# Gate and up products in 32-token groups on four column strips, with VectorE turning the activations

## The chip, the core and the metric

The kernel runs on one core of a Trainium2 chip. The time is that of one execution on the device in microseconds, and a kernel's time is the median of its runs. All arithmetic is float32.

## What is computed

One layer over 1024 latent tokens of width 1024: a mixer (a linear recurrence and gated linear attention), a LayerNorm, and then the part that matters here, a mixture of 32 experts of which each token takes 4:

```python
logits = xt @ w_router + b_router
top_v, top_i = lax.top_k(logits, 4);  top_w = softmax(top_v)
# for the tokens of expert e:
gate = min(xb @ w_gate[e] + b_gate[e], 7)
up   = clip(xb @ w_up[e] + b_up[e], -7, 7)
act  = (up + 1) * gate * sigmoid(1.702 * gate)
y    = (act @ w_down[e] + b_down[e]) * row_weight      # added to the token's row
```

Each of w_gate[e], w_up[e] and w_down[e] is 1024 x 1024, 4 MB. The last LayerNorm follows.

## The kernel before

The mixer, the router and the construction of the job table take the first 669 us of the profile. Then comes the expert loop, with which the change deals.

**Jobs.** A job is up to 128 tokens of one expert. The table is built on the chip. Job u has a type from 1 to 4, the number of quarters (32 tokens) in use; `J_FIRST` says that it is the first job of its expert, and `J_ORD` the expert's ordinal. An expert's first job is the partial one; jobs of type 4 with the same weights may follow. For these inputs there are 49 jobs of 32 experts. By the matmuls of the trace their types are, from u = 0: 4 4 3 2 4 2 4 3 | 1 4 2 3 2 4 4 1 | 3 2 2 4 1 3 4 3 | 2 4 4 1 4 4 3 3 | 2 1 4 1 4 4 4 1 | 4 4 4 2 4 2 4 1 | 4. The jobs 1, 4, 6, 9, 13, 14, 19, 25, 26, 28, 34, 36, 37, 40, 44, 46 and 48 are later jobs of their expert; the other 32 are first.

**TensorE.** Its order in iteration u is: first half of gate_up(u), the turn of the activations of u-1, second half of gate_up(u), down(u-1). `gate_up` multiplies the turned tokens `xT` (the stationary operand) with eight pieces of weights `ring[0..7]` (1 MB each; even ones gate, odd ones up, two k tiles of 128 rows in each). It waits for each piece by itself (`d_gu[q]`) and gives it back by itself (`gu_used`). The code for the tokens depends on the type: "full" (128 stationary columns, 512 moving ones), "half" (64 columns, two matmuls side by side on two column strips), "quarter" (32 columns, four matmuls of 256 side by side on four strips); type 3 is half and then quarter. Gate sums lie in PSUM banks 0 and 1, up sums in 2 and 3. `turn` is 2 to 8 transposes on TensorE into banks 4 and 5, which ScalarE (line 1258) and VectorE (line 1870) copy to `aT`. `down` multiplies `aT` with four pieces `ring[8..11]` of w_down into banks 6 and 7, again by full, half or quarter.

**VectorE.** In iteration u: the copy of `aT`; `turn_rows_in` (line 1671, a 32x32 block transpose of the gathered tokens, after the last use of `xT`); `swiglu(u)` (lines 1698 to 1713; bias adds out of PSUM first, which give the banks back through `g_biased` and `gu_free`, one instruction per part of 32 or 64 partitions); `weigh(u-1)` (lines 1645 to 1658) after down(u-1). ScalarE has the sigmoid (line 1270).

**GpSimd.** Gathers the tokens, scatters the results with an add, and spreads the bias rows of an expert over 128 partitions (`partition_broadcast`: line 2039 for gate and up, line 2042 for down).

**SyncE's queue.** In iteration u, in this order: if job u+1 is the first of its expert, its two bias rows and its eight pieces, piece q as soon as gate_up(u) has used its buffer (line 497); if job u is first, its down bias and its four pieces of w_down, piece q as soon as down(u-1) has used it (line 525). The ring holds one expert, so each piece has one buffer.

Of the kernel before, what the change touches and what calls it, by code (L numbers as in the profile page):

```python
# [13 lines left out]
ALU = mybir.AluOpType  # L14
# [23 lines left out]
def layer(nc, x, c, ctx, c_ctx, w_ada, b_ada, w_in, conv_w, conv_b, lru_wa, lru_ba, lru_wx, lru_bx,  # L38
# [28 lines left out]
    GUP, DNP = 8, 4  # L67
# [12 lines left out]
    with ctxs:  # L80
# [162 lines left out]
        ebias = reg(o, 3, D); o += 3072  # L243
        assert o <= AW
        xacc = reg(16384, 2, D)
        brow = adarow[0:1, 0:3, :].rearrange("p a b -> p (a b)")
# [12 lines left out]
        psG, psU = psall[:, 0:2 * BANK], psall[:, 2 * BANK:4 * BANK]  # L259
        psT, psY = psall[:, 4 * BANK:6 * BANK], psall[:, 6 * BANK:8 * BANK]  # L260
# [4 lines left out]
        JOB_KINDS = {4: (FULL, 0, D), 3: (HALF + QUARTER, 0, BANK + QW), 2: (HALF, 0, BANK), 1: (QUARTER, BANK, BANK + QW)}  # L265
# [43 lines left out]
        d_bias, d_bdn, bias_spread, bdn_spread = sem("d_bias"), sem("d_bdn"), sem("bias_spread"), sem("bdn_spread")  # L309
# [4 lines left out]
        act_turned, aT_act, aT_dve = sem("act_turned"), sem("aT_act"), sem("aT_dve")  # L314
# [115 lines left out]
        def _(sp):  # L430
# [90 lines left out]
            def dn_pieces(e, u):  # L521
                for q in range(DNP):
                    sp.wait_ge(dn_used, DNP * u + (q + 1))
                    w_v = w_down[0].rearrange("e (q c p) n -> e q p c n", c=2, p=P)[:, q]
                    sp.dma_start(ring[GUP + q], w_v[ds(e, 1)].rearrange("a p c n -> p (a c) n")).then_inc(d_dn[q], 16)

            def bias_rows(e):
                for g, b_v in enumerate((b_gate, b_up)):
                    sp.dma_start(brow[:, g * D:(g + 1) * D], b_v[0][ds(e, 1)]).then_inc(d_bias, 16)

            def down_row(e):
                sp.dma_start(brow[:, 2 * D:3 * D], b_down[0][ds(e, 1)]).then_inc(d_bdn, 16)
# [5 lines left out]
            with sp.Fori(0, OUTER) as o4:  # L538
                live = sp.value_load(tab[0:1, ds(o4 * (INNER * NC) + J_LIVE, 1)], min_val=0, max_val=1)
                with sp.If(live > 0):  # L540
                    with sp.Fori(0, INNER) as i4:
                        u = o4 * INNER + i4
                        nxt = sp.value_load(tab[0:1, ds(u * NC + (2 * NC + J_FIRST), 1)], min_val=0, max_val=1)
                        with sp.If(nxt > 0):
                            e = sp.value_load(tab[0:1, ds(u * NC + (2 * NC + J_E), 1)], min_val=0, max_val=NE - 1)
                            spread = sp.value_load(tab[0:1, ds(u * NC + (NC + J_ORD), 1)], min_val=16, max_val=16 * NE)
# [3 lines left out]
                            gu_pieces(e, u)  # L550
# [18 lines left out]
        def gate_up(pe, kind, u, order_, k0, k1, first=False):  # L569
            if k0 == 0:  # L570
                pe.wait_ge(xT_ready, u + 1)
            sweeps = {4: ("full",), 3: ("half", "quarter"), 2: ("half",), 1: ("quarter",)}[kind]
            for sweep in sweeps:
                for q in range(k0, k1):
                    g = q % 2
                    if q < 2 and sweep == sweeps[0]:
                        if g == 0 and not first:
                            pe.wait_ge(g_biased, u)
                        if g == 1:
                            pe.wait_ge(gu_free, u + 1)  # L580
                    if sweep == sweeps[0]:
                        pe.wait_ge(d_gu[q], order_)
                        if kind < 4:
                            settle(pe)
                    for k in (2 * (q // 2), 2 * (q // 2) + 1):
                        w = ring[q][:, k % 2]
                        if sweep == "full":
                            for s in range(2):
                                mm = pe.matmul(ps[2 * g + s], xT[:, k, :], w[:, s * BANK:(s + 1) * BANK],  # L589
                                               start=(k == 0), stop=(k == KD - 1))  # L590
                        if sweep == "half":
                            for j in range(2):
                                mm = pe.matmul(ps[2 * g][HT * j:HT * j + HT, :], xT[:, k, 0:HT], w[:, j * BANK:(j + 1) * BANK],  # L593
                                               start=(k == 0), stop=(k == KD - 1), skip_group_check=True)
                        if sweep == "quarter":
                            r = slice(QUARTER_AT[kind], QUARTER_AT[kind] + QR)
                            for j in range(4):
                                mm = pe.matmul(ps[2 * g + 1][QR * j:QR * j + QR, 0:QW], xT[:, k, r], w[:, j * QW:(j + 1) * QW],  # L598
                                               start=(k == 0), stop=(k == KD - 1), skip_group_check=True)
                    if sweep == sweeps[-1]:  # L600
                        mm.then_inc(gu_used, 1)

        def down(pe, kind, u, order_):
            pe.wait_ge(aT_act, u + 1)
            pe.wait_ge(aT_dve, u + 1)
            pe.wait_ge(y_biased, u + 1)
            sweeps = {4: ("full",), 3: ("half", "quarter"), 2: ("half",), 1: ("quarter",)}[kind]
            for sweep in sweeps:
                for k in range(KD):
# [9 lines left out]
                    if sweep == "half":  # L619
                        for j in range(2):  # L620
                            mm = pe.matmul(ps[6][HT * j:HT * j + HT, :], aT[:, k % 4, HT * (k // 4):HT * (k // 4) + HT],  # L621
                                           w[:, j * BANK:(j + 1) * BANK],
                                           start=(k == 0), stop=(k == KD - 1), skip_group_check=True)
# [31 lines left out]

# [1491 lines left out]
```

## Time and profile before

| what | value |
|---|---|
| median of 3 runs | 2295.06 us (2294.68 to 2297.74) |
| the profiled execution | 2291.36 us, its span 2289.3 us |
| TensorE matmul busy | 2155.0 us, 94% |
| VectorE / ScalarE / GpSimd busy | 45% / 21% / 20% |
| weights and all else moved | 512.34 MB, mean 224 GB/s |

The page's busy shares are means over the whole span. The expert loop runs from 669 us to 2270 us. In the chain of waits each row is work that the end waited for; in the timeline, the number in brackets is how long the engine stood idle before the row and what ended that. A float32 matmul shows as two records.

### The profile page before, as it was taken

To read this page: it belongs to the slowest core of one execution; us is meant where nothing else is said; L and a number is where in the kernel's file an instruction comes from. 1 tells how busy PE (TensorE), PEld (TensorE's weight loads), DVE (VectorE), ACT (ScalarE), POOL (GpSimd) and SP (SyncE) were. 2 spreads that over 40 slices of the span, in tenths; PEclk is the share of its full clock that TensorE was granted. 3 is DMA by queue.
4 is the path that set the end of the run, shared out by engine and by line. 5 is a ranking of instruction groups with operands and counts; after the bars stand their busy time and mean duration, and the time that the engine had idled before them with its cause. 6 is when DMAs were issued, how large, how long until landed. Compare 5 with 4: busy or idle time off the path is not lost.

```text
span 2289.3 us, 35330 instructions
## 1 busy us (share of the span) xinstructions
PE 2155.0 (94%) x9863; PEld 998.5 (44%) x9864; DVE 1023.8 (45%) x1586; ACT 479.0 (21%) x647; POOL 465.4 (20%) x427
## 2 busy tenths in 40 slices
PE   6999999789959999999998899999999999999995
PEld 3544444554544444443443344444443444444442
DVE  2765656557782442444335343333254332222346
ACT  2343347422210111111111111111111111111134
POOL 1011100202311221223122232212113212212212
PEclk9999999789969999999999999999999999999998
DMA  9222320032256767789479999747899648897673
GB/s 351 84 69 70 101 74 19 1 114 83 83 194 213 270 246 239 249 332 374 158 281 401 340 369 403 255 163 254 306 371 348 236 160 271 296 314 247 204 283 128
DMA packets 169785, 512.34 MB, mean 224 GB/s; under 512 B 16815, under 2 KB 51383, under 8 KB 168586
## 3 DMA queue, kind: packets, MB, share of 16 engines
q1 hardware_dynamic: 152290, 468.96, 54.9%
q0 software_dynamic: 15840, 37.45, 7.4%
q10 hardware_dynamic: 1608, 5.29, 0.6%
q8 instruction: 30, 0.49, 0.1%
q14 instruction: 17, 0.14, 0.0%
HBM read 482.08 MB, written 32.51 MB: 225 GB/s over the span
## 4 chain that ended last, share of the span: by engine, by line
PE 86%; DVE 6%; DMA 3%; SPq 2%; issue 2%; ACT 1%; POOLq 0%; DVEq 0%; POOL 0%; ACTq 0%
PE psall L589 27%; PE psall L617 14%; PE psall L593 10%; PE psall L774 9%; PE psall L621 5%; PE psall L598 4%; PE psall L762 3%; PE psall L881 2%; PE psall L875 2%; DMA arena<-in_w_down_dram 2%; PE psall L626 2%; PE psall L658 1%; PE psall L741 1%; SPq L438 1%; DVE arena L1498 1%
## 5 line engine op out<-in xcount | busy, mean ns | idle before, releaser
L589 PE MATMUL psall<-arena 128*128 128x512 f32 x1472 | 645.1, 596 | 23.7 <-issue 18.9
L589 PEld LDWEIGHTS psall<-arena 128*128 128x128 f32 x1472 | 278.4, 191 | 368.8 <-issue 362.4
L617 PE MATMUL psall<-arena 128*128 128x512 f32 x736 | 322.6, 596 | 5.2 <-issue 2.8
L593 PE MATMUL psall<-arena 128*64 128x512 f32 x1152 | 256.1, 595 | 6.2 <-DMA arena<-in_w_up_dram 2.1
L1671 DVE STREAM_TRANSPOSE arena<-arena 128x1024 f32<-128x1024 f32 x49 | 61.0, 1245 | 446.7 <-PE psall L589 276.5
L774 PE MATMUL psall<-arena 128*128 128x512 f32 (+1 forms) x560 | 227.1, 562 | 0.0
L617 PEld LDWEIGHTS psall<-arena 128*128 128x128 f32 x736 | 139.2, 191 | 183.0 <-issue 181.2
L1258 ACT COPY arena<-psall 128x512 f32<-128x512 f32 x49 | 28.7, 586 | 724.5 <-PE psall L658 724.5
L1870 DVE COPY arena<-psall 128x512 f32<-128x512 f32 x48 | 33.2, 691 | 313.7 <-PE psall L658 307.1
L1270 ACT ACTIVATE arena<-arena 128x1024 f32<-128x1024 f32 x49 | 51.8, 1057 | 571.1 <-DVE arena L1698 571.1
L1991 POOL DMA_INDIRECT arena<-h_rows,lruw x144 | 147.6, 1025 | 82.6 <-POOL lruw L1984 39.7
L1653 DVE TENSOR_TENSOR arena<-psall,arena 32x256 f32<-32x256 f32 (+2 forms) x122 | 78.6, 645 | 189.0 <-PE psall L617 137.2
L593 PEld LDWEIGHTS psall<-arena 128*64 128x64 f32 x1152 | 83.2, 137 | 162.6 <-issue 162.6
L774 PEld LDWEIGHTS psall<-arena 128*128 128x128 f32 x560 | 106.3, 190 | 109.1 <-issue 106.1
L1984 POOL COPY lruw<-arena 128x4 int32 (+1 forms) x48 | 9.2, 191 | 658.2 <-DVE arena L1671 620.2
L621 PE MATMUL psall<-arena 128*64 128x512 f32 x576 | 129.3, 595 | 13.4 <-DMA arena<-in_w_down_dram 11.1
L598 PE MATMUL psall<-arena 128*32 128x256 f32 x2048 | 117.3, 381 | 1.9 <-issue 1.9
L2005 POOL DMA_INDIRECT stream_rows<-arena,lruw x56 | 91.6, 1636 | 93.6 <-DMA stream_rows<-arena,lruw 44.9
L1658 DVE SCALAR_TENSOR_TENSOR arena<-arena,lruw,adarow 32x256 f32<-32x256 f32 (+2 forms) x122 | 90.8, 744 | 6.6
L598 PEld LDWEIGHTS psall<-arena 128*32 128x32 f32 x2048 | 64.0, 110 | 59.7 <-issue 22.2
L621 PEld LDWEIGHTS psall<-arena 128*64 128x64 f32 x576 | 41.7, 137 | 97.8 <-issue 97.8
L2039 POOL PARTITION_BROADCAST arena<-adarow x31 | 75.3, 2428 | 29.4 <-issue 16.2
(336 smaller groups left out, 2120.7 us busy)
## 6 DMA issues: line engine op xcount, KB each, us to landing
arena<-in_w_gate_dram SPq DMA_DIRECT2D x128, 1024.0 KB, 6.7
arena<-in_w_up_dram SPq DMA_DIRECT2D x128, 1024.0 KB, 7.4
arena<-in_w_down_dram SPq DMA_DIRECT2D x128, 1024.0 KB, 9.2
arena<-in_w_ada_dram SPq DMA_DIRECT2D x16, 1024.0 KB, 5.2
arena<-in_w_ada_dram SPq DMA_DIRECT2D x4, 2048.0 KB, 14.5
arena<-in_x_dram SPq DMA_DIRECT2D x16, 512.0 KB, 7.0
arena<-in_w_in_dram SPq DMA_DIRECT2D x16, 512.0 KB, 4.1
arena<-in_w_out_dram SPq DMA_DIRECT2D x1, 4096.0 KB, 13.9
```

The costliest lines, as they stand in the source:

```text
L589: mm = pe.matmul(ps[2 * g + s], xT[:, k, :], w[:, s * BANK:(s + 1) * BANK], start=(k == 0), stop=(k == KD - 1))
L593: mm = pe.matmul(ps[2 * g][HT * j:HT * j + HT, :], xT[:, k, 0:HT], w[:, j * BANK:(j + 1) * BANK], start=(k == 0), stop=(k == KD - 1), skip ...
L598: mm = pe.matmul(ps[2 * g + 1][QR * j:QR * j + QR, 0:QW], xT[:, k, r], w[:, j * QW:(j + 1) * QW], start=(k == 0), stop=(k == KD - 1), skip ...
L617: mm = pe.matmul(ps[6 + s], aT[:, k, :], w[:, s * BANK:(s + 1) * BANK], start=(k == 0), stop=(k == KD - 1))
L621: mm = pe.matmul(ps[6][HT * j:HT * j + HT, :], aT[:, k % 4, HT * (k // 4):HT * (k // 4) + HT], w[:, j * BANK:(j + 1) * BANK], start=(k == ...
L762: mm = pe.matmul(ps[i % JB][:, :], uT[:, k, j * P:(j + 1) * P], wv[:, k, :], start=(k == 0), stop=(k == KD - 1))
L774: mm = pe.matmul(ps[i % JB][0:w, 0:seg[1] - seg[0]], wring[n % WRING][:, k, 0:w], uT[:, k, seg[0]:seg[1]], start=(k == 0), stop=(k == KD - 1))
L1653: mm = dve.tensor_tensor(yb[p0:p1, c:c + n], psY[p0:p1, c:c + n], ebias[p0:p1, 2, b:b + n], ALU.add)
L1658: mm = dve.scalar_tensor_tensor(out=yb[p0:p1, c:c + n], in0=yb[p0:p1, c:c + n], scalar=(wcolq if c else wcol)[p0:p1], in1=adarow[p0:p1, 3, ...
L1991: pool.indirect_dma_start(out=xg[:, CW * t:CW * (t + 1)], out_offset=None, in_=h2_dram.rearrange("a (j n) -> (a j) n", n=CW), in_offset=ba ...
L2005: return pool.indirect_dma_start(out=to, out_offset=bass.IndirectOffsetOnAxis(ap=index, axis=0), in_=yb[:, cols], in_offset=None, bounds_c ...
L2039: pool.partition_broadcast(ebias[:, 0:2].rearrange("p a n -> p (a n)"), brow[:, 0:2 * D]).then_inc(bias_spread, 16)
```

## The change

`gate_up` has one form for all types. Tokens go in groups of 32: group t has the stationary columns 32t to 32t+31 and PSUM bank t. Each matmul has 512 moving columns, 256 of gate and 256 of up, and four of them stand side by side on four column strips. The loop over k runs in two sweeps of four k tiles; a sweep waits for four pieces at once, runs the groups in use (nested tests on the type) and gives the four back together. `gate_up` waits for `gu_free` (both bias adds of the job before) ahead of its first matmul; `g_biased` is no longer waited for there.

The turn on TensorE and the copies by ScalarE and VectorE are gone. VectorE turns the activations by 32x32 blocks, straight to `aT`, after `weigh(u-1)`; w_down's rows are read in another order to match (two adjacent rows, 8 KB, for each partition and piece).

The bias adds of `swiglu` are one instruction each for all types. The bias rows of gate and up come by DMAs that write 128 partitions; they are issued behind the eight pieces and a wait for `gu_free`, and GpSimd spreads only the down bias.

```diff
 def gu_pieces(e, u):
     for q in range(GUP):
-        if u is not None:
-            sp.wait_ge(gu_used, GUP * u + (q + 1))
+        if u is not None and q % 4 == 0:
+            sp.wait_ge(gu_used, NPAIR * u + (q // 2 + 2))
         ...
 def dn_pieces(e, u):
     for q in range(DNP):
         sp.wait_ge(dn_used, DNP * u + (q + 1))
-        w_v = w_down[0].rearrange("e (q c p) n -> e q p c n", c=2, p=P)[:, q]
+        w_v = w_down[0].rearrange("e (p q c) n -> e q p c n", q=DNP, c=2)[:, q]
 ...
 def bias_rows(e):
     for g, b_v in enumerate((b_gate, b_up)):
-        sp.dma_start(brow[:, g * D:(g + 1) * D], b_v[0][ds(e, 1)]).then_inc(d_bias, 16)
+        rows = b_v[0][ds(e, 1)].rearrange("a (j n) -> (a j) n", j=4)
+        sp.dma_start(ebq[:, g], rows.unsqueeze(1).to_broadcast([4, QR, QW])).then_inc(d_bias[g], 16)
 ...
-                            sp.wait_ge(bias_spread, spread)
-                            settle(sp)
-                            bias_rows(e)
                             gu_pieces(e, u)
+                            sp.wait_ge(gu_free, u + 2)
+                            bias_rows(e)
 ...
+        def gate_up(pe, groups, u, order_, m0, m1):
+            if m0 == 0:
+                pe.wait_ge(xT_ready, u + 1)
+                pe.wait_ge(gu_free, u + 1)
+            for m in range(m0, m1, 2):
+                for q in range(2 * m, 2 * m + 4):
+                    pe.wait_ge(d_gu[q], order_)
+                    settle(pe)
+                def group(t):
+                    for k in range(2 * m, 2 * m + 4):
+                        for j in range(4):
+                            mm = pe.matmul(psGU[QR * j:QR * j + QR, t], xT[:, k, QR * t:QR * t + QR],
+                                           wpair[k // 2][:, :, k % 2, QW * j:QW * j + QW],
+                                           start=(k == 0), stop=(k == KD - 1), skip_group_check=True)
+                    return mm
+                with pe.If(groups > 1):
+                    with pe.If(groups > 2):
+                        with pe.If(groups > 3):
+                            group(3)
+                        group(2)
+                    group(1)
+                group(0).then_inc(gu_used, 2)
 ...
 def down(pe, kind, u, order_):
-    pe.wait_ge(aT_act, u + 1)
-    pe.wait_ge(aT_dve, u + 1)
+    pe.wait_ge(aT_ready, u + 1)
     pe.wait_ge(y_biased, u + 1)
 ...
-                            by_kind(pe, t, lambda kind: gate_up(pe, kind, u, on_, 0, GUP // 2))
+                            with pe.If(t > 0):
+                                gate_up(pe, t, u, on_, 0, NPAIR)
                             tp, op_ = typ_of(pe, typ_p), ord_of(pe, ord_p, wait_p)
-                            with pe.If(tp > 0):
-                                pe.wait_ge(act_ready, u + 1)
-                                by_kind(pe, tp, lambda kind: turn(...).then_inc(act_turned, 1))
-                            by_kind(pe, t, lambda kind: gate_up(pe, kind, u, on_, GUP // 2, GUP))
                             by_kind(pe, tp, lambda kind: down(pe, kind, u, op_))
 ...
+        def swiglu(u, groups):
+            dve.wait_ge(gu_used, u * NPAIR + NPAIR)
+            dve.wait_ge(d_bias[0], order_)
+            dve.tensor_tensor(gv, psGU[:, 0:groups, 0], bias[0], ALU.add).then_inc(g_biased, 1)
+            dve.wait_ge(d_bias[1], order_)
+            dve.wait_ge(aT_ready, u + 1)
+            dve.scalar_tensor_tensor(out=uv, in0=psGU[:, 0:groups, 1], scalar=1.0, in1=bias[1],
+                                     op0=ALU.add, op1=ALU.add).then_inc(gu_free, 1)
 ...
+        def turn_activations(u, groups):
+            dve.wait_ge(act_ready, u + 2)
+            dve.wait_ge(dn_used, u * DNP + DNP)
+            dve.transpose(aT[:, :, 0:QR * groups].rearrange("p b (t s) -> p t b s", s=QR),
+                          ub[:, 0:QW * groups].rearrange("p (t i b) -> p t b i", i=QR, b=KD)).then_inc(aT_ready, 1)
 ...
                                     by_kind(dve, tp, lambda kind: weigh(u, kind, orderp))
+                                    by_kind(dve, typ_of(dve, typ_c), lambda groups: turn_activations(u, groups))
```

## Rows read from the trace of the kernel before

**Rows 1.** The page: busy time, and the chain that ended last, by engine.

```profile
PE 2155.0 (94%) x9863; PEld 998.5 (44%) x9864; DVE 1023.8 (45%) x1586; ACT 479.0 (21%) x647; POOL 465.4 (20%) x427
...
PE 86%; DVE 6%; DMA 3%; SPq 2%; issue 2%; ACT 1%; POOLq 0%; DVEq 0%; POOL 0%; ACTq 0%
```

**Rows 2.** The expert loop's TensorE groups by form: busy, mean ns, idle before and releasers.

```profile
L589 PE MATMUL psall<-arena 128*128 128x512 f32 x1472 | 645.1, 596 | 23.7 <-issue 18.9 <-DVE arena L1698 4.8
...
L593 PE MATMUL psall<-arena 128*64 128x512 f32 x1152 | 256.1, 595 | 6.2 <-DMA arena<-in_w_up_dram 2.1 <-issue 1.7 <-DVE arena L1698 0.8
L621 PE MATMUL psall<-arena 128*64 128x512 f32 x576 | 129.3, 595 | 13.4 <-DMA arena<-in_w_down_dram 11.1 <-issue 2.2
...
L658 PE MATMUL psall<-ident,arena 128*128 128x128 f32 x288 | 41.0, 278 | 2.5 <-DVE arena L1713 2.5
```

**Rows 3.** The chain in order of time: start, us, what (jobs 29 to 31).

```profile
1597.84 13.97 PE psall L589 x32
1612.68 13.74 PE psall L589 x32
...
1640.15 7.02 PE psall L593 x32
1647.17 3.59 PE psall L598 x64
```

**Rows 4.** The page's group of the quarter's weight loads.

```profile
L598 PEld LDWEIGHTS psall<-arena 128*32 128x32 f32 x2048 | 64.0, 110 | 59.7 <-issue 22.2
```

**Rows 5.** TensorE's timeline behind quarter sweeps (jobs 8 and 9).

```profile
964.40 7.09 PE L621 MATMUL psall<-arena 128*64 128x512 f32 x32 [1.53 <-issue]
...
976.01 13.97 PE L589 MATMUL psall<-arena 128*128 128x512 f32 x32 [0.93 <-issue]
```

**Rows 6.** What SyncE's queue waited for: total, times, longest.

```profile
SPq L497 <- PE psall L589: 446.2, 125, 33.5
```

**Rows 7.** Line 497 (the pieces) from 1845 to 1875 us, time to landing.

```profile
DMA to landing us min/median/max: 4.8/5.2/5.8
```

**Rows 8.** TensorE's timeline from 1259 to 1278 us; five like rows lie between.

```profile
1259.86 1.94 PE L593 MATMUL psall<-arena 128*64 128x512 f32 x8 [0.61 <-DMA arena<-in_w_up_dram]
...
1277.53 1.94 PE L621 MATMUL psall<-arena 128*64 128x512 f32 x8 [1.01 <-DMA arena<-in_w_down_dram]
```

**Rows 9.** Busy time by stretch, the granted clock, DMA share and GB/s.

```profile
8.00:14.00 6.00, 1.52 (x9) 0.44 (x13) 1.57 (x3) 1.40 (x2) 2.63 (x4) 1.00 1.01 419
...
1220.00:1230.00 10.00, 9.21 (x46) 3.57 (x46) 9.02 (x15) 2.99 (x3) 2.38 (x1) 1.00 1.03 405
```

**Rows 10.** VectorE's groups by form.

```profile
L1671 DVE STREAM_TRANSPOSE arena<-arena 128x1024 f32<-128x1024 f32 x49 | 61.0, 1245 | 446.7 <-PE psall L589 276.5 <-PE psall L598 97.5 <-PE psall L593 61.0
...
L1658 DVE SCALAR_TENSOR_TENSOR arena<-arena,lruw,adarow 32x256 f32<-32x256 f32 x64 | 31.4, 491 | 1.7
L1658 DVE SCALAR_TENSOR_TENSOR arena<-arena,lruw,adarow 64x512 f32<-64x512 f32 x36 | 31.1, 864 | 2.3
...
L1698 DVE TENSOR_TENSOR arena<-psall,arena 128x1024 f32<-128x1024 f32 x23 | 27.3, 1187 | 1.1 <-PE psall L589 1.1
...
L1653 DVE TENSOR_TENSOR arena<-psall,arena 32x256 f32<-32x256 f32 x64 | 26.9, 420 | 2.4 <-issue 1.6
...
L1653 DVE TENSOR_TENSOR arena<-psall,arena 64x512 f32<-64x512 f32 x36 | 24.8, 689 | 49.4 <-PE psall L626 27.4 <-POOLq L2067 15.7 <-PE psall L621 5.4
```

**Rows 11.** TensorE's timeline at the second job and at the end of the loop.

```profile
712.86 16.50 PE L589 MATMUL psall<-arena 128*128 128x512 f32 x32 [4.49 <-DVE arena L1698]
...
2251.22 1.09 PE L658 MATMUL psall<-ident,arena 128*128 128x128 f32 x8 [2.48 <-DVE arena L1713]
2253.91 15.67 PE L617 MATMUL psall<-arena 128*128 128x512 f32 x32 [1.60 <-ACT arena L1260]
```

**Rows 12.** TensorE's busy time and granted clock behind the wait ahead of 712.86.

```profile
714.00:718.00 4.00, 4.00 (x6) 0.51 0.45 145
```

**Rows 13.** Waits of VectorE for GpSimd between 1640 and 1800 us.

```profile
DVE arena L1653 <- POOLq L2067: 15.7, 2, 9.7
```

More of the change, by code:

```diff
@@ L242, in layer @@
         yb = reg(o, D); o += 1024
-        ebias = reg(o, 3, D); o += 3072
+        ebq = reg(o, 2, QW); o += 512
+        ebd = reg(o, D); o += 1024
         assert o <= AW
         xacc = reg(16384, 2, D)
-        brow = adarow[0:1, 0:3, :].rearrange("p a b -> p (a b)")
+        wpair = [reg(4096 * m, 2, 2, D) for m in range(NPAIR)]
+        brow = adarow[0:1, 2, :]
         mod2 = ada1[:, :, :, :].rearrange("p a b c -> p (a b c)")[:, 0:2 * KD].rearrange("p (s k) -> p s k", s=2)
@@ L566, in _ @@
             sp.wait_ge(late_out, 48)
-        def gate_up(pe, kind, u, order_, k0, k1, first=False):
-            if k0 == 0:
+        def gate_up(pe, groups, u, order_, m0, m1):
+            if m0 == 0:
                 pe.wait_ge(xT_ready, u + 1)
[L572 to L601, printed above, removed]
@@ L620, in down @@
                         for j in range(2):
[L621 removed]
+                            mm = pe.matmul(ps[6][HT * j:HT * j + HT, :], aT[:, k, 0:HT],
                                            w[:, j * BANK:(j + 1) * BANK],
@@ L654, in ord_of @@
             return eng.snap(bounded, min_val=16, max_val=16 * NE)
-        def turn(pe, src, n, first=0):
-            for k in range(first, n):
-                mm = pe.transpose(psT[:, k * P:(k + 1) * P], src[:, k * P:(k + 1) * P], ident[:, :])
-            return mm
         @block.tensor
@@ L976, in _ @@
             t0, o0 = typ_of(pe, typ_p), ord_of(pe, ord_p, wait_p)
-            by_kind(pe, t0, lambda kind: gate_up(pe, kind, 0, o0, 0, GUP // 2, True))
+            gate_up(pe, t0, 0, o0, 0, NPAIR // 2)
             job_lists()
-            by_kind(pe, t0, lambda kind: gate_up(pe, kind, 0, o0, GUP // 2, GUP))
+            gate_up(pe, t0, 0, o0, NPAIR // 2, NPAIR)
             with pe.Fori(0, OUTER) as o4:
@@ L1641, in weigh @@
             def weigh(u, kind, order_):
-                parts, lo, hi = JOB_KINDS[kind]
+                parts = DOWN_PARTS[kind]
                 dve.wait_ge(y_dve, u + 1)
@@ L1690, in finish @@
                                          op0=ALU.mult, op1=ALU.add).then_inc(fin_ready, 1)
-            def swiglu(u, kind):
-                parts, lo, hi = JOB_KINDS[kind]
+            def swiglu(u, groups):
                 s7 = 1.0 / (1.0 + math.exp(-SWIGLU * LIMIT))
-                dve.wait_ge(gu_used, u * GUP + GUP)
-                dve.wait_ge(bias_spread, order_)
-                for p0, p1, c, b, n in parts:
-                    mm = dve.tensor_tensor(gb[p0:p1, c:c + n], psG[p0:p1, c:c + n], ebias[p0:p1, 0, b:b + n], ALU.add)
-                mm.then_inc(g_biased, 1)
-                for p0, p1, c, b, n in parts:
-                    mm = dve.scalar_tensor_tensor(out=ub[p0:p1, c:c + n], in0=psU[p0:p1, c:c + n], scalar=1.0,
-                                                  in1=ebias[p0:p1, 1, b:b + n], op0=ALU.add, op1=ALU.add)
-                mm.then_inc(gu_free, 1)
-                w = slice(lo, hi)
+                w = slice(0, QW * groups)
+                gv, uv = (v[:, w].rearrange("p (t n) -> p t n", t=groups) for v in (gb, ub))
+                bias = [ebq[:, g].unsqueeze(1).to_broadcast([P, groups, QW]) for g in range(2)]
+                dve.wait_ge(gu_used, u * NPAIR + NPAIR)
[5 more added lines that the diff above has]
+                                         op0=ALU.add, op1=ALU.add).then_inc(gu_free, 1)
                 dve.wait_ge(gu_free, u + 2)
@@ L1916, in _ @@
                                     dve.nop()
+                                dve.nop()
+                            with dve.Else():
+                                by_kind(dve, typ_of(dve, typ_c), lambda groups: turn_activations(u, groups))
                                 dve.nop()
```

57 lines of the change are left out of this document (17 added, 40 removed).

## The prediction, made before the changed kernel ran

> **What bounds the kernel now.** I read the page first: TensorE is busy 94% of the span, and the chain that ended last is TensorE's for 86% [rows 1]. The other engines lie beside it. Then the groups by form: the first group of the expert loop waits 23.7 us, of which one "issue" of 13.5 us precedes the loop, the half forms wait 19.6 us, and 13.2 of these are named as DMA's; for more than 1000 us of matmuls TensorE hardly stands [rows 2]. The chain in order of time shows the loop as matmul blocks end to end [rows 3]. This could mislead: an expert's 12 MB take about as long as a small job's matmuls, so I looked at what SyncE's queue waits for. It is TensorE's use of the buffers [rows 6]: one buffer per piece, so the moment at which a piece is given back decides when the next expert's comes. Between 1200 and 1280 us, where experts with one small job follow each other, DMA is full and the waits for it lie [rows 8, 9]. So there are two bounds: TensorE over most of the loop, DMA in runs of small jobs.
>
> **TensorE's work.** A half gate_up of a full job is 32 records in 13.74 us, 429 ns for each pass of 512 columns. The half form takes 7.02 us for 16 such passes of two strips, 439 ns; the quarter form 3.59 us for 16 passes of 256 columns on four strips, 224 ns, that is 11 ns over half of 427 [rows 3]. The new form has four strips and 512 columns: 427 + 11 = 438 ns, like the half form. A group is 16 passes, 7.02 us, so gate_up is 28.08 us for type 4 (before 27.46), 21.06 for 3 (21.22), 14.04 for 2 (14.04), 7.02 for 1 (7.18). With 23, 8, 10 and 8 jobs: +14.3 - 1.3 - 1.3 = **+11.7 us**. These are 2304 passes, so the bounds are far: 429 ns a pass, as in the full form, makes it 21 us less, and 448 ns 23 us more. I take the row with strips, since it is the nearest.
>
> The turns go. Their group is 41.0 us busy [rows 2], but overlaps its neighbours at both ends; between two halves the chain loses 1612.68 - 1597.84 - 13.97 = 0.87 us for eight transposes [rows 3], and 0.2 to 1.0 for the others. Summed over the 48 turns inside the loop: **-35 us** (bounds -30 and -41).
>
> Full-width and strip matmuls now alternate in every pair of jobs. A block after another width shows 13.97 instead of 13.73 us [rows 3]; for 23 full downs I take 0.2 us ahead and 0.15 behind, less those that had it before, and less 0.2 where a full gate_up followed a strip down: **+2.5 us** (0 to 8). The Trainium skill says that changing the tiling mode drains TensorE (TensorEngine Tiling (Array Packing), Key Properties); the trace agrees, with these 0.2 us.
>
> Behind quarter sweeps TensorE stands 0.2 to 1.5 us for "issue" [rows 5]: 28 ns an instruction leaves its sequencer no lead at a jump. The new groups run at 55 ns an instruction; the waits ahead of down go, those after a quarter down stay, and the nested tests there cost, by my guess, 0.15 us more each; no row shows them. 16 x 0.5 saved, 16 x 0.15 added: **-5.6 us** (-8 to +5). Sum of TensorE's own work: 11.7 - 35 + 2.5 - 5.6 = **-26 us**.
>
> **When the weights come.** A piece asked for with idle engines lands after 4.8 us [rows 7]. In a full stretch, seven waits in a row end within 1277.53 - 1259.86 = 17.67 us, 2.9 us a piece [rows 8], gathers and scatters included; at 405 GB/s [rows 9] a piece (1.05 MB) alone is 2.6. I take 2.8 us a piece and, at the same rate, 0.33 us of DMA time for each quarter (128 KB) that a job gathers, and again for its scatter. With these I kept an account of the 49 jobs: blocks of TensorE by the durations above, each piece in the queue when its buffer is free, landed 2.8 us after the one before, and a block not before its pieces. By the rules of before it finds 17 us of waits in the right places (jobs 17, 18 and 32, 33), and runs parallel to the ends of the blocks in the trace within some 2 us. So it may be trusted with the new rules.
>
> Before, piece q came back after q/8 of gate_up; now four after the first half and four at the end. The second lot is asked for when gate_up(u) ends, and its last piece lands 4.8 + 3 x 2.8 = 13.2 us later. TensorE needs it after down(u-1) and half of gate_up(u+1). Job 35 (type 1, behind a down of type 1): 3.6 + 0.8 + 3.5 = 7.9 us, so it waits **5.3**. Jobs 20 and 47: 7.0 + 3.5, **2.7** each. Job 10: 11.4, **1.8**. After a full down (13.8 us) nothing waits. Sum 12.5, before none.
>
> The runs: take 15 to 18. From the end of job 15's gate_up TensorE has 14.0 + 21.1 + 4.3 = 39.4 us of work ahead of job 17's first sweep. DMA must by then bring what is left of job 16's eight pieces (6.7, as the first lot was asked for 3.5 us before), four of w_down and the first four of job 17: 14.7 x 2.8 = 41.2, + 1.4 to land, + 3.4 for gathers and scatters: 46.0. Wait 6.6. Before, the first matmul there needed one piece of the four, not all. Carried on: 20.6 us of waits in jobs 17 and 18; 4.2 in job 12; 7.8 in jobs 22 and 24; 15.5 in jobs 32 and 33. Sum 48 us, before 17. DMA has no less to move there, so these runs keep nothing of TensorE's gain, and begin later.
>
> Together 60.5 against 17: **+43 us**. I take off half of what w_down might gain: it now moves 8 KB per partition at a stretch; in the one stretch that loads 8 KB rows (w_ada) the rate was 419 GB/s against 405 [rows 9], some 4% of a third of the pieces, 4.5 us in the account, where it binds; half: **-2 us**. The new bias DMAs (256 packets of 1 KB for each expert) stand in the account with 0.6 us.
>
> **The edges.** gate_up(u+1) now needs both bias adds: turn_rows_in 1.25 and two adds of 1.19 us, with semaphores 3.9 us after gate_up(u) [rows 10], against a down of 3.6 at least: 0.2 us in five places, +1, and +1.2 at job 1, where TensorE already waits 4.49 us [rows 11]. At the last job the swiglu ends at 2251.2; the turn must now wait for weigh(47), 4 x 0.42 + 4 x 0.49 + 0.2 = 3.8 us [rows 10], and then takes 1.25: down(48) at 2256.3 instead of 2253.9 [rows 11]: +2.4. Elsewhere the turn is covered: weigh (3.8 us for a quarter, 6.9 with two halves of 0.69 and 0.86 besides) and turn (1.25 us for all, less for fewer groups; double if its strided read halves the rate) against a gate_up of 7 us at least, 14 behind most downs of type 3. If that cover went, down would wait. The bias adds of types 1 to 3, GpSimd's broadcast and the copies lie beside TensorE: 0. **+4 us**.
>
> **The sum.** -26 + 43 - 2 + 4 = +19. Some waits fall where TensorE is late anyhow; with all of it in one account the total is 3 us less: **+16 us**.
>
> After the wait of 4.49 us the granted clock was 0.51 for 4 us, the level of 1.2 GHz, and the block took 16.50 us instead of 13.9 [rows 11, 12]. Waits of 5 us and more come five times now; two precede work that decides: up to +5, in the range only.
>
> Own time 2291.4 + 16 = 2307.4; the median of the runs is 3.7 above the profiled execution: **2311 us**.
>
> **Rivals.**
> *The lots flow faster (ends faster).* Asked for four at a time, pieces come at 2.6 us instead of 2.8. For: 419 GB/s in [rows 9] is 2.5 us; the queue never runs dry within a lot. Against: with the queue full in the loop, it came to 405 GB/s and 2.9 us a piece [rows 8, 9]. At 2.6 us the account gives 23 us less, so -7: **2288**; it decides below 2.67 us a piece. Chance 0.20.
> *Gain and waits cancel.* 2.7 us a piece gives 14 us less, passes of 430 ns some 16 (2304 x 8 ns, less what waits take back): +2 or 0, **2297**. Chance 0.15.
> *VectorE is late with aT.* weigh(u-1) may wait for GpSimd's scatter, 9.7 us once [rows 13], and the turn now stands behind it. It decides where gate_up(u+1) is of type 1 (eight jobs), from a lateness of some 3 us on; with 3 us beyond that in five of them +15: **2326**. Against: GpSimd loses 2.4 us of broadcast per expert. Chance 0.08.
> *The loads of the weights are not covered.* The quarter form has 64 loads of 110 ns within 3.59 us [rows 3, 4], so they overlap there. If at 512 columns they cost 27 ns more a pass (as one 110 ns load in four): 2304 x 27 = +62, less some 20 of waits that vanish: **2353**. Chance 0.04. The Trainium skill has a rule of this kind, that a weight load overlaps a running matmul only if it is for other rows of the array (TensorE: Matmul & The Clock Gate, Part 3); all four strips use the same rows, yet the rows above show the overlap.
> My forecast has 0.53.
>
> **The numbers.** The forecast's own range is 2301 to 2323. With the rivals, VectorE's included and the loads left out: 2284 to 2327. A change within 0.2% (4.6 us) can't be told from none. Faster: the first rival, 0.20; the same: the second, 0.15; slower: forecast, VectorE, loads, 0.65.
>
> **What would show it.** Gate_up blocks of 28.1 us for type 4 and 7.0 per group; no line 658; waits of TensorE for w_gate and w_up of 40 to 60 us in sum (jobs 12, 17, 18, 22, 33, 35, 47), ended by DMA; DMA idle early in each gate_up; down(48) some 2.4 us later. The prediction is wrong if the DMA waits sum to under 30 us (the first rival), if a pass is not 438 ns, or if down waits for VectorE's turn in the middle of the loop.

## The result

| kernel | median | runs |
|---|---|---|
| before | 2294.87 us | 2294.48 to 2297.74 |
| changed | 2371.26 us | 2370.16 to 2373.26 |

The ratio is 1.0331, 95% interval [1.0313, 1.0349]: 76.4 us slower. Slower was the side that I gave 0.65, but the time lies 44 us beyond the range.

### The profile page after: what moved, and what is told of

Read it like the earlier page. It is cut to its first block, busy times and chain, and to the rows that moved or that the text cites. A ratio compares the mean times of both kernels' runs of the same rounds, so it can differ in the third digit from the quotient of the medians.

```text
span 2371.5 us, 42832 instructions
## 1 busy us (share of the span) xinstructions
PE 2147.2 (91%) x14119; PEld 853.9 (36%) x14120; DVE 977.9 (41%) x1439; ACT 388.4 (16%) x549; POOL 391.2 (16%) x395
## 2 busy tenths in 40 slices
DMA packets 161716, 520.39 MB, mean 219 GB/s; under 512 B 17007, under 2 KB 59767, under 8 KB 144138
## 4 chain that ended last, share of the span: by engine, by line
PE 73%; DMA 12%; DVE 6%; SPq 5%; issue 2%; ACT 1%; DVEq 0%; POOLq 0%; POOL 0%
PE psall L582 37%; PE psall L608 12%; PE psall L761 9%; DMA arena<-in_w_up_dram 8%; DMA arena<-in_w_down_dram 4%; PE psall L749 3%; PE psall L868 2%; PE psall L612 2%; PE psall L862 2%; SPq L499 2%; PE psall L728 1%; SPq L532 1%; SPq L440 1%; DVE arena L1474 1%; PE psall L618 1%
## 5 line engine op out<-in xcount | busy, mean ns | idle before, releaser
L582 PE MATMUL psall<-arena 128*32 128x512 f32 x9216 | 1032.7, 607 | 111.2 <-DMA arena<-in_w_up_dram 73.0
L582 PEld LDWEIGHTS psall<-arena 128*32 128x32 f32 x9216 | 313.4, 112 | 818.7 <-issue 818.5
L1647 DVE STREAM_TRANSPOSE arena<-arena 128x1024 f32<-128x1024 f32 x49 | 61.0, 1245 | 807.4 <-PE psall L582 796.5
L608 PE MATMUL psall<-arena 128*128 128x512 f32 x736 | 323.9, 598 | 10.0 <-DVE arena L1694 8.7
L608 PEld LDWEIGHTS psall<-arena 128*128 128x128 f32 x736 | 138.4, 191 | 195.4 <-issue 183.9
L612 PE MATMUL psall<-arena 128*64 128x512 f32 x576 | 131.1, 597 | 19.3 <-DMA arena<-in_w_down_dram 18.7
L761 PEld LDWEIGHTS psall<-arena 128*128 128x128 f32 x560 | 106.3, 190 | 109.1 <-issue 106.1
L612 PEld LDWEIGHTS psall<-arena 128*64 128x64 f32 x576 | 40.1, 136 | 109.9 <-issue 109.8
L1694 DVE STREAM_TRANSPOSE arena<-arena 128x1024 f32<-128x1024 f32 (+3 forms) x49 | 76.5, 1562 | 1.0
L1980 POOL COPY lruw<-lruw 128x1 int32 x40 | 7.4, 184 | 417.3 <-DVE arena L1634 381.4
L749 PE MATMUL psall<-arena 128*128 128x512 f32 x160 | 70.0, 592 | 0.0
L1941 POOL TENSOR_TENSOR arena<-arena 128x1280 f32<-128x1280 f32 x8 | 23.2, 2904 | 268.6 <-ACT arena L1071 268.6
L618 PE MATMUL psall<-arena 128*32 128x256 f32 x1024 | 60.1, 380 | 1.5 <-issue 0.8
L868 PE MATMUL psall<-arena 128*128 128x512 f32 x128 | 59.3, 618 | 0.0
```

What stands on the lines that cost most here:

```text
L582: mm = pe.matmul(psGU[QR * j:QR * j + QR, t], xT[:, k, QR * t:QR * t + QR], wpair[k // 2][:, :, k % 2, QW * j:QW * j + QW], start=(k == 0) ...
L608: mm = pe.matmul(ps[6 + s], aT[:, k, :], w[:, s * BANK:(s + 1) * BANK], start=(k == 0), stop=(k == KD - 1))
L612: mm = pe.matmul(ps[6][HT * j:HT * j + HT, :], aT[:, k, 0:HT], w[:, j * BANK:(j + 1) * BANK], start=(k == 0), stop=(k == KD - 1), skip_gro ...
L618: mm = pe.matmul(ps[7][QR * j:QR * j + QR, 0:QW], aT[:, k, r], w[:, j * QW:(j + 1) * QW], start=(k == 0), stop=(k == KD - 1), skip_group_c ...
L749: mm = pe.matmul(ps[i % JB][:, :], uT[:, k, j * P:(j + 1) * P], wv[:, k, :], start=(k == 0), stop=(k == KD - 1))
L761: mm = pe.matmul(ps[i % JB][0:w, 0:seg[1] - seg[0]], wring[n % WRING][:, k, 0:w], uT[:, k, seg[0]:seg[1]], start=(k == 0), stop=(k == KD - 1))
```

## The profile after

The page, with the chain of waits by engine below the busy times:

```profile
span 2371.5 us, 42832 instructions
...
PE 2147.2 (91%) x14119; PEld 853.9 (36%) x14120; DVE 977.9 (41%) x1439; ACT 388.4 (16%) x549; POOL 391.2 (16%) x395
...
DMA packets 161716, 520.39 MB, mean 219 GB/s; under 512 B 17007, under 2 KB 59767, under 8 KB 144138
...
PE 73%; DMA 12%; DVE 6%; SPq 5%; issue 2%; ACT 1%; DVEq 0%; POOLq 0%; POOL 0%
...
L582 PE MATMUL psall<-arena 128*32 128x512 f32 x9216 | 1032.7, 607 | 111.2 <-DMA arena<-in_w_up_dram 73.0
...
L608 PE MATMUL psall<-arena 128*128 128x512 f32 x736 | 323.9, 598 | 10.0 <-DVE arena L1694 8.7
...
L612 PE MATMUL psall<-arena 128*64 128x512 f32 x576 | 131.1, 597 | 19.3 <-DMA arena<-in_w_down_dram 18.7
...
L618 PE MATMUL psall<-arena 128*32 128x256 f32 x1024 | 60.1, 380 | 1.5 <-issue 0.8
```

TensorE's share of the chain falls from 86% [rows 1] to 73%; DMA rises from 3 to 12%, SyncE's queue from 2 to 5%. The bytes moved are 520.39 MB for 512.34: 8 MB or 1.6% more, the 32 x 256 KB of the bias DMAs. What grew is the idle time ahead of the loop's matmuls. Before, the four groups of [rows 2] and three smaller ones had 54.0 us, 13.5 of them ahead of the loop, so 40; now it is 111.2 + 10.0 + 19.3 + 1.5, less 14.6 ahead of the loop: 127 us. The forecast had +47 of such waits (43 for weights, 4 at the edges), and +87 came.

TensorE's timeline from 1245 to 1315 us, where small jobs of new experts follow each other; rows between are left out:

```profile
1248.13 9.98 PE L582 MATMUL psall<-arena 128*32 128x512 f32 x64 [10.40 <-DMA arena<-in_w_up_dram]
1259.09 7.07 PE L582 MATMUL psall<-arena 128*32 128x512 f32 x64 [0.98 <-DMA arena<-in_w_up_dram]
...
1285.60 10.02 PE L582 MATMUL psall<-arena 128*32 128x512 f32 x64 [6.65 <-DMA arena<-in_w_up_dram]
1296.63 7.07 PE L582 MATMUL psall<-arena 128*32 128x512 f32 x64 [1.00 <-DMA arena<-in_w_up_dram]
...
1314.99 27.67 PE L582 MATMUL psall<-arena 128*32 128x512 f32 x256 [0.72 <-issue]
```

These are jobs 17 and 18, of type 2. Each has one long wait for pieces, ahead of its first sweep, and the same 64 matmuls that take 7.07 us take 10.0 behind it. The windows say why (us, busy time of PE, weight loads, VectorE, ScalarE and GpSimd, granted clock, DMA share, GB/s):

```profile
1244.00:1248.00 4.00, 0.00 (x0) 0.00 (x0) 1.13 (x1) 0.00 (x0) 1.82 (x2) 0.50 1.02 410
1248.00:1252.00 4.00, 3.87 (x20) 0.99 (x24) 0.00 (x0) 0.00 (x0) 0.00 (x0) 0.50 1.06 378
1252.00:1256.00 4.00, 4.00 (x32) 1.00 (x28) 0.00 (x0) 0.00 (x0) 0.00 (x0) 0.74 0.81 301
```

While TensorE stands, the granted clock falls to 0.50, the level of 1.2 GHz, and it is back only some 6 us after the work is (0.74 is the mean of 0.50 and full speed in the last window). A wait of 10 us costs 13.

SyncE's queue from 1273 to 1290 us, each row one DMA and how long its issue held the queue:

```profile
1273.77 2.84 SPq L499 DMA_DIRECT2D arena<-in_w_gate_dram  x1
1276.70 2.38 SPq L499 DMA_DIRECT2D arena<-in_w_up_dram  x1
1279.33 2.22 SPq L532 DMA_DIRECT2D arena<-in_b_gate_dram  x1
1281.65 4.66 SPq L532 DMA_DIRECT2D arena<-in_b_up_dram  x1
...
1289.73 2.98 SPq L527 DMA_DIRECT2D arena<-in_w_down_dram  x1
```

The two bias DMAs, 256 KB, held the queue for 6.9 us in this full stretch, more than the 5.2 us of the two 1 MB pieces ahead of them. That is not the 0.6 us of my account. What they do by themselves can be seen where the queue runs dry behind them:

```profile
761.00:763.00 2.00, 2.00 (x6) 0.90 (x5) 0.00 (x0) 0.00 (x0) 0.00 (x0) 1.00 0.94 368
763.00:765.00 2.00, 2.00 (x15) 0.47 (x17) 1.09 (x1) 0.00 (x0) 0.00 (x0) 1.00 0.30 103
765.00:767.00 2.00, 2.00 (x24) 0.65 (x20) 1.89 (x3) 0.00 (x0) 0.07 (x1) 1.00 0.09 29
```

The pieces end at 368 GB/s; then the last 103 x 2 + 29 x 2 = 264 KB, about the size of the two bias DMAs, trickle at a third of that and less, and the share of the DMA engines that are busy, the number ahead of the GB/s, is 0.30 and 0.09. Why these packets don't fill the 16 engines isn't said there: their size, their number and the source (each kilobyte is read 32 times) are new at once. Nor does the profile say how much of the 76 us hangs on it.

## The experiments

Two suspects were left: the lots of four pieces (the forecast's +43) and the bias DMAs (the forecast's 0.6). The first four runs take them one by one.

**Four sweeps of two k tiles.** Waits and releases by two pieces in place of four.

```diff
-if u is not None and q % 4 == 0:
-    sp.wait_ge(gu_used, NPAIR * u + (q // 2 + 2))
+if u is not None and q % 2 == 0:
+    sp.wait_ge(gu_used, NPAIR * u + (q // 2 + 1))
 ...
-for m in range(m0, m1, 2):        # q, k in range(2 * m, 2 * m + 4)
+for m in range(m0, m1):           # q, k in range(2 * m, 2 * m + 2)
```

> The changed kernel with four sweeps of two k tiles instead of two sweeps of four: each sweep waits for two pieces and gives two back. Theory A (the coarse lots cost what is missing): the waits for w_gate and w_up, 73 us in the changed kernel, fall by more than half, and the time by 30 to 45 us, to about 2330. Theory B (something else in the weight traffic, the bias DMAs or the order of w_down's rows, makes DMA slower): the waits stay above 50 us and the time falls by less than 15.

2325.27 us, ratio 1.0138 [1.0118, 1.0158]: 46 us less than the changed kernel. The group's idle time says where:

```profile
L582 PE MATMUL psall<-arena 128*32 128x512 f32 x9216 | 1016.5, 599 | 76.3 <-DMA arena<-in_w_up_dram 40.9 <-issue 23.5 <-DVE arena L1678 11.9
...
L612 PE MATMUL psall<-arena 128*64 128x512 f32 x576 | 134.5, 613 | 20.0 <-DMA arena<-in_w_down_dram 19.9
```

The waits for w_up fall by 32 us; those for w_down, which come behind the bias DMAs in the queue, stay. The time met the 30 to 45 us of theory A; the waits for w_up fell by 44%, not by more than half. Lots are a cause, but not alone.

**The bias DMAs behind w_down's pieces.**

```diff
 gu_pieces(e, u)
-sp.wait_ge(gu_free, u + 2)
-bias_rows(e)
 ...
 dn_pieces(ed, u)
+sp.wait_ge(gu_free, u + 2)
+bias_rows(eb)                     # where the next job has a new expert
```

> The changed kernel with one step of SyncE's queue moved: the two bias DMAs of the next expert are issued behind the four pieces of w_down, not ahead of them. Theory C (a bias DMA of 256 small rows holds SyncE's queue for up to 7 us while the queue is full, and w_down's issue behind it comes late): 15 to 30 us faster, about 2350. Theory A: within 5 us of the changed kernel.

2357.88 us, ratio 1.0273 [1.0253, 1.0293]: 13 us less, between the marks of the two theories (15 to 30, and under 5). Now w_down hardly waits (2.5 us), but w_up waits 81.9 instead of 73.0. The place in the queue decides who waits for the bias DMAs, not whether.

**The bias DMAs cut down.**

```diff
-sp.dma_start(ebq[:, g], rows.unsqueeze(1).to_broadcast([4, QR, QW]))
+sp.dma_start(ebq[0:4, g], rows)
```

> The changed kernel, but the bias DMAs write four partitions instead of 128 (the other partitions keep what was there, so the bias of gate and up is left out there). It takes both the hold of the queue and the DMA work of 8 MB in 1 KB packets away. Theory C: like bias_last or some 5 us better. If the 1 KB packets themselves are what slows the full stretches (360 GB/s against 398 before), it is 10 us and more better than bias_last.

2307.39 us, ratio 1.0055 [1.0036, 1.0074]: 64 us less, in one line, and 50 us less than with the bias DMAs behind w_down. It leaves out the gate and up biases in 124 of 128 partitions. The groups:

```profile
L582 PE MATMUL psall<-arena 128*32 128x512 f32 x9216 | 1018.4, 601 | 87.6 <-DMA arena<-in_w_up_dram 50.7 <-issue 28.9 <-DVE arena L1678 8.0
...
L612 PE MATMUL psall<-arena 128*64 128x512 f32 x576 | 127.8, 596 | 0.6 <-DMA arena<-in_w_down_dram 0.6
```

Against the changed kernel, 23.6 and 18.7 us of waits are gone, and 14.3 and 3.3 us of busy time of the same matmuls too: the clock lost behind the waits. Together 60 of the 64 us.

**w_down's rows in the old order.** The old `rearrange` of `dn_pieces`, 4 KB rows.

> The changed kernel with w_down read in the order of before, 4 KB rows, two for a partition (so the rows don't match the turned activations: the last product has its rows in another order). Theory D (8 KB rows 32 KB apart come slower than 4 KB rows that follow each other): 10 to 25 us faster. My prediction: 2 to 4 us slower.

2374.75 us, ratio 1.0353 [1.0335, 1.0371]. The 8 KB rows may be worth 3.5 us; the intervals overlap, so no more than a hint.

Then, why 256 KB cost so much.

**The same packets from distinct rows.** Each of the 128 packets of 1 KB reads a kilobyte of its own.

```diff
-rows = b_v[0][ds(e, 1)].rearrange("a (j n) -> (a j) n", j=4)
-sp.dma_start(ebq[:, g], rows.unsqueeze(1).to_broadcast([4, QR, QW]))
+rows = (w_gate, w_up)[g][0][ds(e, 1), 0:QR].rearrange("a r (j n) -> (a r j) n", j=4)
+sp.dma_start(ebq[:, g], rows)
```

> The changed kernel, but each bias DMA reads 128 different pieces of 1 KB (32 rows of the expert's w_gate or w_up, so the biases are other numbers) instead of four pieces 32 times each. Size, number and target of the packets stay. If the size and number of packets make the bias DMAs dear, it stays at about 2371. If it is that 32 packets read the same kilobyte, it comes near to bias_small, about 2310.

2315.61 us, ratio 1.0087 [1.007, 1.0104]. Same bytes, same size and number of packets, same places written: 56 of the 64 us are gone. Where the queue runs dry, the tail is short:

```profile
763.00:765.00 2.00, 2.00 (x18) 0.55 (x20) 1.39 (x2) 0.00 (x0) 0.00 (x0) 1.00 0.14 47
765.00:767.00 2.00, 2.00 (x24) 0.65 (x20) 2.00 (x2) 0.00 (x0) 0.19 (x1) 1.00 0.00 0
```

So it is neither the size of the packets nor their count. But two things differ between these DMAs: the changed kernel's read each kilobyte 32 times, and they name their source as four rows (`[4, QR, QW]`), the others as 128. At the first expert the pair of bias DMAs has the queue to itself. From 671 to 676 us, in slices of 0.125 us, the share of the 16 DMA engines that are busy, in tenths (9 is 90% and more), in the changed kernel and then here:

```profile
DMA  0000000002001122222222231222272222110000
DMA packets 266, 0.29 MB, mean 57 GB/s; under 512 B 8, under 2 KB 264, under 8 KB 264
```

```profile
DMA  0000086479959930050000000000000000000000
DMA packets 290, 0.29 MB, mean 57 GB/s; under 512 B 32, under 2 KB 288, under 8 KB 288
```

The changed kernel's pair keeps a quarter of the engines busy, about four of 16, for 3 us; the pair from distinct rows keeps up to 90% and more busy and is through in half of that. The small packets say the same: 8 for two DMAs, four each, against 32, 16 each. In windows of half a microsecond (the last three numbers are the granted clock, the DMA share and the GB/s):

```profile
673.00:673.50 0.50, 0.00 (x0) 0.00 (x0) 0.50 (x1) 0.00 (x0) 0.00 (x0) 0.50 0.26 94
```

```profile
672.00:672.50 0.50, 0.00 (x0) 0.00 (x0) 0.47 (x2) 0.00 (x0) 0.00 (x0) 0.50 0.86 256
```

An engine that is busy moves 94 / (0.26 x 16) = 23 GB/s in the first and 256 / (0.86 x 16) = 19 in the second. So the repeated reading itself does not slow it here; the DMA is slow because it runs on about four engines. That puts 64 KB on each of the four, as much as one of 16 engines carries of a whole 1 MB piece, and the pieces behind it in the queue go over all 16 (a share of 1.02 where they come one after another). That the four comes from the four rows of the source is likely; no run changes that number alone. Issuing one of these DMAs took longer too, 0.62 and 0.57 us at the median against 0.35 and 0.41 here.

**The kernel before with lots of four.** Its own gate_up, only released and waited for by four pieces.

```diff
-if u is not None:
-    sp.wait_ge(gu_used, GUP * u + (q + 1))
+if u is not None and q % 4 == 0:
+    sp.wait_ge(gu_used, GUP * u + (q + 4))
 ...
-if sweep == sweeps[0]:
-    pe.wait_ge(d_gu[q], order_)
+if sweep == sweeps[0] and q == k0:
+    for z in range(4):
+        pe.wait_ge(d_gu[q + z], order_)
```

> The kernel before with the coarse lots alone: gate_up waits for four pieces at once, and SyncE asks for the next four when the fourth has been used. All else as before. My account of the lots gives 43 us of waits more, of which some 5 are absorbed: 30 to 45 us slower than before, about 2330. If the lots matter only together with the bias DMAs: under 15 us slower.

2323.39 us, ratio 1.012 [1.0104, 1.0137]: +29 us from lots alone, just under the 30 to 45 that I expected.

**Both kernels with light weights.** Each piece loads 64 KB instead of 1 MB, so that TensorE waits for hardly any.

```diff
-sp.dma_start(ring[q], w_v[ds(e, 1)].rearrange("a p c n -> p (a c) n"))
+sp.dma_start(ring[q][:, 0:1, 0:128], w_v[ds(e, 1)].rearrange("a p c n -> p (a c) n")[:, 0:1, 0:128])
```

> The changed kernel with every piece of weights cut to 512 bytes per partition (1/16 of the traffic; the rest of each buffer keeps old numbers), so that TensorE doesn't wait for weights. Together with b_light it gives TensorE's own work: my prediction is 26 us less than before, and 4 us more at the edges, so 22 us under b_light. With passes of 431 ns, as the changed kernel shows, 30 us and more under.

> The kernel before with the same cut of the weight pieces. Its 27 us of waits for DMA go: about 2270.

The changed kernel 2250.47 us (0.9808 [0.9791, 0.9824]), the kernel before 2281.56 (0.9939 [0.9923, 0.9956]). The change's compute side is worth -31.1 us, and before lost only 13 us to its waits for weights; I had expected 25 for it (2270 us).

**Biases spread on the chip.** Rows of 4 KB, GpSimd's broadcast as before, and ScalarE puts the strips into place; then the same with sweeps of two k tiles, and for comparison those sweeps with the bias DMAs cut down.

```diff
-sp.dma_start(ebq[:, g], rows.unsqueeze(1).to_broadcast([4, QR, QW])).then_inc(d_bias[g], 16)
+sp.dma_start(brow2[:, g * D:(g + 1) * D], b_v[0][ds(e, 1)]).then_inc(d_bias, 16)
 ...
+pool.partition_broadcast(ebw.rearrange("p a n -> p (a n)"), brow2).then_inc(bias_spread, 16)
 ...
+for j in range(4):
+    act.copy(ebq[QR * j:QR * j + QR], ebw[QR * j:QR * j + QR, :, QW * j:QW * j + QW]).then_inc(bias_strips, 4)
```

> The changed kernel, except that an expert's gate and up biases come as they did before: one row of 4 KB each from HBM ahead of the weight pieces, spread over the partitions by GpSimd, and then copied by ScalarE, in four small instructions, into the strips' layout. The output is the reference's. Theory 'the re-read bias rows cost it' (the DMAs that read the same kilobyte 32 times over take DMA time from the weights): about what the kernel gained with the bias DMAs cut down to four partitions, 2307 us, so 2300 to 2315. Rival 'bias data of 512 KB for each expert has to come somewhere; what was saved in the cut kernel was work left out': 2330 us and over, since GpSimd's spreading (some 4 us) and the copies then come late for the first job of an expert. In the trace the DMA should read about as many bytes as before, and the idle time before gate and up products should be near 90 us, not 111.

> The same as the run before it, and gate and up products in four sweeps of two k tiles in place of two sweeps of four, so that two pieces are waited for and released at a time. If coarse lots and re-read bias rows are together all that the change lost, this is under the kernel before: lots of two gave 46 us, but with the bias DMAs gone less of it is left to gain, so 2265 to 2290 us, with the w_up waits at most 40 us in sum. If the two savings are the same waits seen twice, it stays at 2295 to 2307.

> Four sweeps of two k tiles, and bias DMAs that write only 4 partitions each, so that most strips add stale numbers (the output is another). It has the same lots as the kernel before it and no spreading by GpSimd or copies by ScalarE: within 5 us of that kernel if the way over GpSimd and ScalarE is free, 10 us or more below it if VectorE waits for that way at the first job of each expert.

| kernel | median | ratio |
|---|---|---|
| spread on the chip | 2312.19 us | 1.0056 [1.0037, 1.0074] |
| the same, sweeps of two | 2281.45 us | 0.9923 [0.9906, 0.9939] |
| cut down, sweeps of two | 2273.90 us | 0.9889 [0.9871, 0.9907] |

(The kernel before had 2299.49 us beside these three.) The first has the ratio of the cut-down kernel with lots of four, 1.0055, so the saving was not work left out. Nor was it SyncE's wait for `gu_free` ahead of the bias DMAs, which that kernel has and this one has not. The second computes all of the reference and is 0.8% faster than the kernel before. Its groups:

```profile
L586 PE MATMUL psall<-arena 128*32 128x512 f32 x9216 | 1011.9, 596 | 54.9 <-issue 23.8 <-DMA arena<-in_w_up_dram 20.2 <-DVE arena L1700 10.8
...
L616 PE MATMUL psall<-arena 128*64 128x512 f32 x576 | 129.4, 596 | 5.0 <-DMA arena<-in_w_down_dram 2.9 <-DVE arena L1716 1.6 <-issue 0.4
```

Waits for w_up have gone from 73.0 to 20.2 us, and "issue", most of it the one wait ahead of the loop, now leads. The third lies 7.6 us below the second, between my two marks of 5 and 10, so whether VectorE waits for the way over GpSimd and ScalarE stays open within those; in the traces it is the waits of these groups, 73.6 us against 65.8, and 7.1 of that are for w_up. With sweeps of two the bias DMAs were worth 51 us (2325.27 - 2273.90; 57 by the ratios) and not 64: the two savings overlap in part.

**One re-reading DMA in the kernel before.** Of the change only this DMA, with its source of four rows, and the wait for `gu_free` ahead of it, into a region that nobody reads:

```diff
 gu_pieces(e, u)
+sp.wait_ge(gu_free, u + 2)
+sp.wait_ge(d_extra, spread)
+rows = b_gate[0][ds(e, 1)].rearrange("a (j n) -> (a j) n", j=4)
+sp.dma_start(ebx[:, 0], rows.unsqueeze(1).to_broadcast([4, QR, QW])).then_inc(d_extra, 16)
```

> The kernel before, with nothing of the change but one DMA more for each expert: the DMA of the gate biases in the changed kernel's form (128 packets of 1 KB, each kilobyte of HBM read 32 times), issued behind the gate and up pieces into a region that nobody reads. The output is the reference's. It is one of the two bias DMAs that the changed kernel has. Theory 'reading the same kilobytes again holds up the weights, whatever the schedule': half of some 56 us if all of it falls on waits, and less where the finer lots of this kernel give slack, so +12 to +28 us. Rival 'the price is there only together with coarse lots of two sweeps': under +5 us. Price of the bytes alone, which the prediction used: +0.3 us for each expert at most, under +5 us too.

2319.73 us against 2295.64, ratio 1.0107 [1.009, 1.0124]: +24 us for 128 KB an expert, 0.8 us each time, with fine lots and a schedule that hardly waited.

```profile
L634 PE MATMUL psall<-arena 128*64 128x512 f32 x576 | 134.1, 611 | 24.7 <-DMA arena<-in_w_down_dram 24.0 <-issue 0.6
```

The same group had 13.4 us of waits, 11.1 of them for w_down [rows 2]: the pieces behind the new DMA are late. So the price is there without the coarse lots, though this run tells nothing of reading against engines. It has a rival of its own: SyncE now waits for `gu_free`, 87.8 us in 26 places. In the small jobs the DMA engines did not run dry for that. SyncE stood for 4.1 us of the stretch from 1222 to 1226 us, and they had work enough (share 1.03, 411 GB/s):

```profile
1222.00:1226.00 4.00, 2.46 (x20) 0.61 (x12) 3.85 (x9) 2.34 (x2) 1.18 (x2) 1.00 1.03 411
```

No run has the wait without the DMA.

## Why the prediction was wrong

Put as steps from run to run, which add up by construction:

| part | forecast | measured | from |
|---|---|---|---|
| compute side with edges | -26 + 4 | -31 | light weights, 2250.47 - 2281.56 |
| waits for weights | +43 - 2 - 3 | +44 | 2307.39 - 2250.47 = 57 now, 2294.53 - 2281.56 = 13 before |
| bias DMAs | in the account with 0.6 us for each expert | +64 | 2371.26 - 2307.39 |
| sum | +16 | +77 (beside its own kernel before: 76.4) | |

**The step that failed** is "The new bias DMAs (256 packets of 1 KB for each expert) stand in the account with 0.6 us." I priced them by bytes at 405 GB/s, the rate of all 16 DMA engines. They run on about four, at some 90 GB/s, and cost 64 us over 32 experts, 2.0 us each; 56 of these go when the same packets come from 128 rows, 8 stay. Unlike other unknown costs it was given no bounds, so the range knew nothing of it. The trace of before has no DMA with such a source, and that should have been said and bounded: w_down's pieces stand right behind these DMAs in a queue that is full in runs of small jobs.

**Weights.** The mechanism of the lots was right: release after half and at the end of gate_up, waits in runs of small jobs, +44 for a forecast of +38. That the sum is so near is partly luck. With the bias DMAs cut down the loop's groups wait 96.9 us, with light weights 50.3, so weights cost 47 us of standing where the account had 60, and 13 in the kernel before where it had 17 (54.0 against 40.8 with light weights). That is +33 for +43; 2.7 us a piece, by my own figure 14 less, would have been about right. What brings the sum back is the clock.

**The clock** was put at up to +5 us. It is more, and goes with the waits: the busy time of gate_up is 1032.7 us in the changed kernel, 1018.4 with the bias DMAs cut down, and with light weights 1005.9:

```profile
L582 PE MATMUL psall<-arena 128*32 128x512 f32 x9216 | 1005.9, 595 | 39.9 <-issue 35.3 <-DVE arena L1678 4.6
```

So 27 us of the changed kernel are clock, and 12.5 of them go with the waits for weights that are left without the bias DMAs. It doesn't take 5 us of standing, the mark that I had set. The timeline has 13 waits of 2.5 to 10.7 us ahead of gate_up in the loop; the rows behind them are 1.3 to 3.0 us too long each, 28 us in sum. One of the short ones:

```profile
1025.28 8.77 PE L582 MATMUL psall<-arena 128*32 128x512 f32 x64 [2.69 <-DMA arena<-in_w_up_dram]
```

These 64 matmuls take 7.07 us elsewhere, and the granted clock was 0.57 from 1025 to 1029 us.

**A pass** of four strips and 512 columns takes 27.67 / 64 = 432 ns behind short waits, not 438. Strips are not slower at all. Blocks of 16, 32, 48 and 64 passes take 7.07, 13.94, 20.81 and 27.67 us: 429 ns for each further pass, and 0.2 us once per block. The two-strip form has the same, 1.94 us for 4 passes and 7.09 for 16, and the full form 13.74 us for 32. My 439 [rows 3] was 429 and the end of a block spread over 16 passes. The new blocks are longer, so 2304 x 6 = 14 us were gained. Against that, the 5.6 us that I took off for "issue" did not come: in the groups of the loop, the wait ahead of it included, it is 32.0 us in the light run of the kernel before and 35.7 in that of the changed one. The 0.15 us for the nested tests was a guess that no run shows by itself, nor do the runs split the rest of the -31. The edges: the first wait ahead of the loop is 1.1 us longer (14.59 for 13.52; the loop begins 4.3 us later, but the matmuls ahead of that wait were 3.3 us late already), and the others stand longer than forecast:

```profile
719.66 30.29 PE L582 MATMUL psall<-arena 128*32 128x512 f32 x256 [6.37 <-DVE arena L1678]
...
2336.14 15.64 PE L608 MATMUL psall<-arena 128*128 128x512 f32 x32 [8.66 <-DVE arena L1694]
```

The first is job 1, 6.4 us for a forecast of 5.7. The second replaces 2.48 + 1.09 + 1.60 = 5.2 us between the last matmul of job 47's down and down(48) [rows 11], so +3.5 for +2.4.

**VectorE's turn** reads with a stride and takes longer than the tokens' turn. By form:

```profile
L1647 DVE STREAM_TRANSPOSE arena<-arena 128x1024 f32<-128x1024 f32 x49 | 61.0, 1245 | 807.4 <-PE psall L582 796.5 <-DMA arena<-h_rows,lruw 10.8 <-DVE small L1754 0.2
...
L1694 DVE STREAM_TRANSPOSE arena<-arena 128x1024 f32<-128x1024 f32 x23 | 47.4, 2062 | 0.6
```

It is covered in the middle of the loop: the page names it for 8.7 us of TensorE's waits, all ahead of the last down.

**The rivals.** None had the cause. The conditions of the second (2.7 us a piece, passes of 430 ns) came about true, and without the bias DMAs it was 2307 and not 2297, for the clock and the edges. VectorE was not late, and the weight loads are covered: 9216 of 112 ns run within passes of 432 ns, though all four strips use the same rows.

## What to carry over

A DMA that spreads a row over many partitions has to be priced by a row of a trace or by a run of its own, not by its bytes; look there at the share of DMA engines that it keeps busy. These kept a quarter busy, and in a full queue they held back the pieces behind them. Where one buffer serves each piece, releases should be as fine as the code allows; going from four pieces to two gave back 31 to 46 us. And a wait of TensorE is to be priced with the clock that it loses: 1.3 to 3.0 us for each wait of 2.5 to 10.7 us here.

## What the runs showed of the hardware

- The bias DMAs of the changed kernel (four source rows, each read by 32 partitions) kept 0.26 to 0.29 of the 16 DMA engines busy and moved 94 to 96 GB/s, so 256 KB took some 3 us. The same 256 packets from 128 rows had a share of up to 0.86 at 256 GB/s. A busy engine moved 19 to 23 GB/s in both. Whether the number of rows decides how many engines work, no run settles.
- SyncE's issue of such a DMA took 0.56 us at the least and up to 7.23 us in a full queue.
- A further pass of 512 float32 columns takes 429 ns with 128, two times 64 or four times 32 stationary columns; a block of passes has some 0.2 us more, once.
- VectorE's 32x32 block transpose of 128x1024 takes 2.06 us with this strided read, and 1.25 us for the tokens.
